# An RWKV-7 / latent-attention / ConvGLU step on one core: sums over a head's channels from split operands, and the final state transposed together with the samples' states

## What is computed

```python
kk = (k * k_k).reshape(B, T, H, N)
kk = kk * lax.rsqrt(jnp.maximum(jnp.sum(kk * kk, axis=-1, keepdims=True), 1e-12))
...
S_T, y = lax.scan(step, wkv0.astype(f32), ...)
mu = jnp.mean(y, axis=-1, keepdims=True)
var = jnp.mean(jnp.square(y - mu), axis=-1, keepdims=True)
y = ((y - mu) * lax.rsqrt(var + GN_EPS)).reshape(B, T, W) * lnx_g + lnx_b
```

## Time and profile before

| | |
|---|---|
| median of 3 runs | 2498.18 us (2497.25 to 2504.71) |
| the profiled execution | 2497.85 us, its span 2496.2 us |
| PE busy | 2431.5 us, 97% of the span |
| DVE busy | 1104.6 us, 44% |
| ACT busy | 870.8 us, 35% |
| mean granted clock of PE | 0.989 of full speed |
| DMA | 284.14 MB, 114 GB/s on average |

### The profile page before, as it was taken

One profiled execution on the slowest core, in us unless ns is written; L12 is line 12 of the kernel. 1 busy time (PEld: TensorE's weight loads), 2 busy tenths in 40 slices (PEclk: granted clock), 3 DMA queues, 4 the chain that ended last, 5 costly groups with the idle time before them and its releaser, 6 DMA issues.

```text
span 2496.2 us, 44147 instructions
## 1 busy us (share of the span) xinstructions
PE 2431.5 (97%) x17372; PEld 2232.2 (89%) x17372; DVE 1104.6 (44%) x1743; ACT 870.8 (35%) x1311; POOL 108.6 (4%) x182
## 2 busy tenths in 40 slices
PE   6999999999899999999998999999999999999997
PEld 6888888888899999999877999999878999999886
DVE  4555656654433322344333544444233444444234
ACT  4444344443323322344223433333222333333232
POOL 4000000000010100000000000000000000000010
PEclk9999999999999999999999999999999999999999
DMA  5323222222533433344533344444333444444433
GB/s 167 105 74 81 78 77 74 74 72 71 132 119 94 124 98 92 96 127 125 169 124 109 112 126 126 126 126 124 127 126 118 132 126 126 126 127 141 128 129 127
DMA packets 414538, 284.14 MB, mean 114 GB/s; under 512 B 31728, under 2 KB 392690, under 8 KB 413536
## 3 DMA queue, kind: packets, MB, share of 16 engines
q1 hardware_dynamic: 405600, 259.16, 35.3%
q0 software_dynamic: 8832, 23.36, 3.4%
HBM read 275.55 MB, written 6.92 MB: 113 GB/s over the span
## 4 chain that ended last, share of the span: by engine, by line
PE 95%; DVE 2%; ACT 1%; DMA 1%; issue 1%; POOL 0%; DVEq 0%; SPq 0%; POOLq 0%; ACTq 0%
PE banks L1453 20%; PE banks L903 19%; PE banks L907 18%; PE banks L904 18%; PE banks L324 2%; PE banks L916 2%; PE banks L918 2%; PE banks L917 2%; PE banks L392 1%; PE banks L1316 1%; PE banks L472 1%; PE banks L1319 1%; PE banks L457 1%; PE banks L1414 1%; PE banks L485 0%
## 5 line engine op out<-in xcount | busy, mean ns | idle before, releaser
L893 DVE TENSOR_TENSOR w_lo<-w_raw,w_hi 128x1024 fp32r<-128x1024 f32 x482 | 590.1, 1225 | 964.5 <-ACT w_hi L888 964.2
L903 PE MATMUL banks<-x_hi,w_hi 128*128 128x384 f32 x2640 | 918.6, 348 | 8.3 <-DVE w_lo L893 8.3
L907 PE MATMUL banks<-x_hi,w_lo 128*128 128x384 f32 x2640 | 886.9, 336 | 0.0
L904 PE MATMUL banks<-x_lo,w_hi 128*128 128x384 f32 x2640 | 885.7, 335 | 0.0
L888 ACT ACTIVATE w_hi<-w_raw 128x1024 fp32r<-128x1024 f32 x482 | 511.3, 1061 | 1039.9 <-PE banks L907 595.5
L903 PEld LDWEIGHTS banks<-x_hi,w_hi 128*128 128x128 f32 x2640 | 497.6, 188 | 35.6 <-issue 11.9
L904 PEld LDWEIGHTS banks<-x_lo,w_hi 128*128 128x128 f32 x2640 | 498.5, 189 | 5.0 <-issue 0.3
L907 PEld LDWEIGHTS banks<-x_hi,w_lo 128*128 128x128 f32 x2640 | 497.6, 188 | 1.2 <-issue 1.2
L1453 PE MATMUL banks<-w_hi,act_hi 128*128 128x512 f32 x528 | 164.2, 392 | 4.6 <-DVE h_rows L2009 2.4
L1453 PE MATMUL banks<-w_lo,act_hi 128*128 128x512 f32 x528 | 164.2, 392 | 0.0
L1453 PE MATMUL banks<-w_hi,act_lo 128*128 128x512 f32 x528 | 163.2, 390 | 0.0
(11 more groups left out here) (401 smaller groups left out, 2294.4 us busy)
## 6 DMA issues: line engine op xcount, KB each, us to landing
w_raw<-in_w_ffn_in SPq DMA_DIRECT2D x176, 512.0 KB, 4.0
w_raw<-in_w_in SPq DMA_DIRECT2D x144, 512.0 KB, 3.8
w_raw<-in_w_ffn_down SPq DMA_DIRECT2D x88, 512.0 KB, 3.6
w_raw<-in_w_out SPq DMA_DIRECT2D x32, 512.0 KB, 3.6
w_raw<-in_w_o_a SPq DMA_DIRECT2D x16, 512.0 KB, 4.0
w_raw<-in_w_o_b SPq DMA_DIRECT2D x16, 512.0 KB, 3.9
w_raw<-in_w_in SPq DMA_DIRECT2D x20, 256.0 KB, 3.8
w_ukv_head<-in_w_ukv POOLq DMA_DIRECT2D x8, 512.0 KB, 3.9
```

The source lines that it names most:

```text
L893: nc.vector.tensor_tensor(lo[:, s], raw[:, s], hi[:, s].bitcast(F32), ALU.subtract).then_inc(lo_done, 1)
L903: nc.tensor.matmul(out, hi[:, s, k, :], xh[:, kt, :], start=kt == 0, stop=False)
L904: nc.tensor.matmul(out, hi[:, s, k, :], xl[:, kt, :], start=False, stop=False)
L907: last = nc.tensor.matmul(out, lo[:, s, k, :], xh[:, kt, :], start=False, stop=kt == 15)
```

## The change

1. The three sums over a head are made of two fp32r products each (`head_sums`), with `bon_r`, an fp32r copy of `BON` that DVE makes once, and with a high part (an ACT copy to fp32r) and a low part (a DVE subtraction) of what is summed. The split operands lie where `m_t`, `c_k` and `c_b` are. ACT counts its three copies of a group in `split_hi`; `kk_sq_done`, `y_raw_done` and `y_sq_done` are now given by DVE, behind the subtraction. Two of ACT's squares are linked, because a copy reads them.
2. The prompt's final state is transposed directly ahead of the samples' states, and its copy stands directly ahead of theirs in ACT's list. The waits for `s_out` and `s0_in` move from ahead of `pe_lora_g` to ahead of `pe_s0`.
3. The numbers of pieces behind `y_ps` are 2, 3, 2, 3, 2 in place of 1, 2, 2, 3, 4.

```diff
--- before.py
+++ after.py
@@ -204,7 +204,16 @@
         be = region("beta", [P, NT])
         kp_ = region("kappa", [P, NT])
         n_t, t_x, t_y, t_g = [region(n, [P, 6, 64]) for n in ("n_t", "t_x", "t_y", "t_g")]
-        t_f, m_t, c_k, c_b = [region(n, [P, 6, P]) for n in ("t_full", "m_t", "c_k", "c_b")]
+        t_f = region("t_full", [P, 6, P])
+        kk_off = top[0]
+        m_t = region("m_t", [P, 6, P])
+        y_off = top[0]
+        c_k = region("c_k", [P, 6, P])
+        var_off = top[0]
+        c_b = region("c_b", [P, 6, P])
+        kk_s = at("square_split", [P, 2, NT], kk_off, F32R)
+        y_s = at("y_split", [P, 2, NT], y_off, F32R)
+        var_s = at("y_square_split", [P, 2, NT], var_off, F32R)
         tok = region("tok_major", [P, 3, 3, P])
         ra = region("r_and_alpha", [P, 5, P])
         un_s = t_y[:, 0:2, :].rearrange("p i c -> p (i c)")
@@ -218,6 +227,7 @@
         so = region("s_out", [64, NB, P])
         st = region("state", [P, 64])
         sto = region("state_rows", [64, P])
+        bon_r = region("bones_r", [P, P], F32R)
         assert top[0] <= 229368, top[0]
         yb, yc, sq_y, rn_y = [t[:, :, :].rearrange("p u c -> p (u c)") for t in (t_g, t_y, n_t, t_x)]
 
@@ -379,9 +389,13 @@
             for k in range(2):
                 nc.tensor.matmul(ps[:, 5, 0:NT], wg[:, k, :], za[:, 2 + k, :], start=k == 0, stop=k == 1)
 
+        def head_sums(out, split):
+            nc.tensor.matmul(out, bon_r[:, :], split[:, 0, :], start=True, stop=False)
+            return nc.tensor.matmul(out, bon_r[:, :], split[:, 1, :], start=False, stop=True)
+
         def pe_kk_sum(f):
             nc.tensor.wait_ge(E("kk_sq_done"), f + 1)
-            nc.tensor.matmul(ps[:, 3, 0:NT], BON, sq[:, :], start=True, stop=True).then_inc(E("kk_sum_ps"), 1)
+            head_sums(ps[:, 3, 0:NT], kk_s).then_inc(E("kk_sum_ps"), 1)
 
         def pe_s0(f):
             for b in range(NB):
@@ -568,29 +582,29 @@
                     last = mm_(ps[heads(i), 5, tile_tok(t)], u_and_p[:, t, 0, heads(i)], c_b[:, 3 * i + t, :],
                                start=False, stop=True, skip_group_check=True)
             last.then_inc(E("y_ps"), 1)
-            pieces(1)
+            pieces(2)
             pe.wait_ge(E("state_done"), f * 4 + 4)
             pe.wait_ge(E("y_raw_done"), f + 1)
-            mm_(ps[:, 3, 0:NT], BON, yb, start=True, stop=True).then_inc(E("mean_ps"), 1)
-            transpose(ps[0:64, 2, 0:P], st[:, :]).then_inc(E("sp_t_ps"), 1)
-            pieces(2)
+            head_sums(ps[:, 3, 0:NT], y_s).then_inc(E("mean_ps"), 1)
+            pieces(3)
             pe.wait_ge(E("sd_done"), f + 1)
             pe.wait_ge(E("y_sq_done"), f + 1)
-            mm_(ps[:, 4, 0:NT], BON, sq_y, start=True, stop=True).then_inc(E("var_ps"), 1)
+            head_sums(ps[:, 4, 0:NT], var_s).then_inc(E("var_ps"), 1)
             if more:
                 pe_kk_sum(f + 1)
             pieces(2)
+            transpose(ps[0:64, 2, 0:P], st[:, :])
             for b in range(NB):
                 last = transpose(ps[0:64, 6 + b // 4, (b % 4) * P:(b % 4 + 1) * P], s0t[:, b, :])
             last.then_inc(E("sd_t_ps"), 1)
             if more:
-                pe.wait_ge(E("s_out"), f + 1)
-                pe.wait_ge(E("s0_in"), f * 32 + 64)
                 pe_lora_g(f + 1)
             pieces(3)
             if more:
+                pe.wait_ge(E("s_out"), f + 1)
+                pe.wait_ge(E("s0_in"), f * 32 + 64)
                 pe_s0(f + 1)
-            pieces(4)
+            pieces(2)
 
         def act_gate_sigmoids(f):
             fn = nc.scalar.activation
@@ -599,9 +613,10 @@
             fn(sw[:, :], ps[:, 2, 0:NT], ACT.Sigmoid, bias=pf[:, 3:4])
             fn(aa[:, :], ps[:, 3, 0:NT], ACT.Sigmoid, bias=pf[:, 4:5]).then_inc(E("sig_done"), 1)
 
-        def act_kk_square(f):
+        def act_kk_square(f, ch):
             nc.scalar.wait_ge(E("kk_raw_done"), f + 1)
-            nc.scalar.activation(sq[:, :], kk0[:, :], ACT.Square).then_inc(E("kk_sq_done"), 1)
+            ch.link(nc.scalar.activation(sq[:, :], kk0[:, :], ACT.Square))
+            nc.scalar.activation(kk_s[:, 0, :], sq[:, :], ACT.Copy).then_inc(E("split_hi"), 1)
 
         def act_exps_early(f):
             fn = nc.scalar.activation
@@ -666,19 +681,18 @@
             act.wait_ge(E("u_ps"), f * 3 + 2)
             fn(un_s[:, :], ps[:, 3, 0:P], ACT.Copy, scale=-1.0).then_inc(E("u_done"), 1)
             if more:
-                act_kk_square(f + 1)
+                act_kk_square(f + 1, ch)
             cut(4)
             if more:
                 act_exps_early(f + 1)
             act.wait_ge(E("yd_ps"), f + 1)
             act.wait_ge(E("y_ps"), f + 1)
-            fn(yb, ps[:, 5, 0:NT], ACT.Copy).then_inc(E("y_raw_done"), 1)
+            fn(yb, ps[:, 5, 0:NT], ACT.Copy)
+            fn(y_s[:, 0, :], ps[:, 5, 0:NT], ACT.Copy).then_inc(E("split_hi"), 1)
             act.wait_ge(E("y_centred"), f + 1)
-            fn(sq_y, yc, ACT.Square).then_inc(E("y_sq_done"), 1)
+            ch.link(fn(sq_y, yc, ACT.Square))
+            fn(var_s[:, 0, :], sq_y, ACT.Copy).then_inc(E("split_hi"), 1)
             cut(5)
-            act.wait_ge(E("sp_t_ps"), f + 1)
-            act.wait_ge(E("states_stored"), OPEN + f)
-            fn(sto[:, :], ps[0:64, 2, 0:P], ACT.Copy).then_inc(E("s_out"), 1)
             if more:
                 act.wait_ge(E("sd_done"), f + 1)
                 act_exps_late(f + 1)
@@ -688,6 +702,8 @@
             if more:
                 act_kk_norm(f + 1, ch)
             act.wait_ge(E("sd_t_ps"), f + 1)
+            act.wait_ge(E("states_stored"), OPEN + f)
+            fn(sto[:, :], ps[0:64, 2, 0:P], ACT.Copy).then_inc(E("s_out"), 1)
             fn(so[:, :, :].rearrange("v (h b) c -> v h (b c)", h=2), ps[0:64, 6:8, :], ACT.Copy)\
                 .then_inc(E("so_done"), 1)
             cut(6)
@@ -737,6 +753,11 @@
         def dve_k_mod(ch):
             ch.link(nc.vector.tensor_scalar(t1[:, :], aa[:, :], -1.0, pf[:, 6:7], ALU.add, ALU.mult))
             ch.link(nc.vector.scalar_tensor_tensor(k2[:, :], t1[:, :], 1.0, z[:, 1, :], ALU.add, ALU.mult))
+
+        def dve_kk_low(f, first=False):
+            nc.vector.wait_ge(E("split_hi"), 1 if first else f * 3 - 1)
+            nc.vector.tensor_tensor(kk_s[:, 1, :], sq[:, :], kk_s[:, 0, :].bitcast(F32), ALU.subtract)\
+                .then_inc(E("kk_sq_done"), 1)
 
         def dve_clamp(f):
             nc.vector.wait_ge(E("kk_sum_ps"), f + 1)
@@ -851,10 +872,16 @@
             tt(s0t[:, :, :], s0t[:, :, :],
                e1[:, 256 + TS - 1:NT:TS].unsqueeze(2).to_broadcast([P, NB, 64]), M).then_inc(E("sd_done"), 1)
 
+            dve.wait_ge(E("split_hi"), f * 3 + 2 + more)
+            tt(y_s[:, 1, :], yb, y_s[:, 0, :].bitcast(F32), S).then_inc(E("y_raw_done"), 1)
+            if more:
+                dve_kk_low(f + 1)
             dve.wait_ge(E("mean_ps"), f + 1)
             stt3(yc, ps[:, 3, 0:NT], -1.0 / 64, yb, M, A).then_inc(E("y_centred"), 1)
             if more:
                 dve_k_mod(ch)
+            dve.wait_ge(E("split_hi"), f * 3 + 3 + more)
+            tt(var_s[:, 1, :], sq_y, var_s[:, 0, :].bitcast(F32), S).then_inc(E("y_sq_done"), 1)
             cut(5)
             if more:
                 dve_kappa(f + 1)
@@ -1550,7 +1577,7 @@
             act_gate_sigmoids(0)
             nc.scalar.preload_act_table_set("natural_log_exp_and_others")
             act_next(T_FT + 2)
-            act_kk_square(0)
+            act_kk_square(0, ch)
             act_exps_early(0)
             act_exps_late(0)
             taken_mixed(T_FT + 2, 2)
@@ -1849,11 +1876,13 @@
             dve_next(T_FT + 1)
             dve_key(0, ch)
             dve.wait_ge(E("tables_in"), 16)
+            cp(bon_r[:, :], BON)
             dve_scan(0, ch)
             dve_centre(ch)
             dve_excl()
             dve_k_mod(ch)
             dve_next(T_FT + 2)
+            dve_kk_low(0, True)
             dve_kappa(0)
             dve_clamp(0)
             dve_bonus_rho(0, ch)
@@ -2085,7 +2114,7 @@
                     ts(ht[:, t, 0:1024], ht[:, t, 0:1024], stat[:, t:t + 1], None, M).then_inc(E("y_ready"), 1)
 
 
-LINKS = {"act_rwkv": 2, "dve_rwkv": 16, "dve_ffn": 3}
+LINKS = {"act_rwkv": 4, "dve_rwkv": 16, "dve_ffn": 3}
 
 _INS = ["x_prompt", "x_sample", "cache_mla_latent", "cache_mla_krope", "state_rwkv_wkv", "state_rwkv_shift",
         "state_ffn_conv", "g_mix", "w_in", "mu_shift", "w0", "w2", "a0", "a2", "g2", "k_k", "k_a", "r_k", "lnx_g",
```

## The result

The changed kernel takes 2547.43 us (2544.97 to 2547.83, 4 runs) where the kernel before takes 2500.39: a ratio of 1.0185, 95% interval 1.0166 to 1.0204. The profiled execution took 2544.97 us against 2497.85, so the two profiles differ by 47.1 us. Forecast were 2525.5 and a range up to 2538: the direction is right, the size is 22 us short, and the time lies 9 us above the range.

The account below looks back on a forecast made before the run. PE, carrying 95% of the chain of waits and gapless in the head groups, was taken as the bound. 7 x 3.5 + 3.2 - 0.3 = 27.4 us on 2497.85 gave 2525.3, as median 2525.5 us; range 2517 to 2538.

Parts of the forecast that it names:

- The new order makes two stalls of 2 us: PE waits 2.0 us at piece 24, 2.1 at piece 28, first of new weight blocks, for their low parts.
- the 0.2 for restarting: In each head group, PE loses 0.2 us for restarting twice, behind the two stalls.
- The sums are worth 0.87 us a group: Three sums over a head on PE each go from 0.64 to 0.35 us, saving 0.87 a group.
- The state's transpose is worth nothing: On PE it takes 0.11 us wherever it stands, so moving it gains nothing by itself.
- A group +3.5, the last +3.2: Each of seven head groups gets 3.5 us longer; the last 3.2, between 2.5 and 3.6.
- Mine are 2.0 and 2.1, so the nearest row speaks against it: Head-group stalls of 2.0 and 2.1 us resemble a 2.2 us wait with clock at 1.00, arguing against clock falls.
- The fall of the clock: Rival: PE's clock falls in the stalls, once per head group, 8 x 1.7 = 13 us more, 2538; chance 0.09.
- the 2.2 us row: Profile row of PE's 2.2 us wait on act_lo, around which the clock stays at 1.00.
- Only one stall: Rival: only one of the head groups' two stalls appears, about 2.2 us less in each group, 2508; chance 0.06.
- a cover that holds: Rival: pieces 24 and 28 find their low parts ready, only the 7 us saving remains, 2491; chance 0.05.
- sums that don't shorten: Rival: new products run like half an old sum, 0.32 us, saving gone, +7, 2532; chance 0.06.
- What would show it: Signs: about fifteen 2 us PE waits on w_lo, 69.2 us groups, sum products 0.175 apart, clock at 1.00.

Follow-up runs that it names:

- 2: Kernel before with only the new order of pieces and of the state's transpose, keeping the old float32 sums: 2541.45 us, ratio 1.0161.
- 4: Changed kernel with the cuts that make the high and low parts for pieces 24 and 28 moved earlier on ACT and DVE: 2493.16 us, ratio 0.9968.
- 8: Changed kernel with piece 24's high part and piece 28's cut made earlier, and one piece moved to the group's end: 2480.36 us, ratio 0.9922.
- 9: Same order as 8, but with the old float32 sums and without the added copies and subtractions: 2485.69 us, ratio 0.9945.
- 3: Kernel before with only the state's transpose, its copy and the two waits moved: 2501.22 us, ratio 1.0011.
- 5: Changed kernel with only the cut for piece 24 moved earlier on ACT and DVE, leaving the second stall: 2515.97 us, ratio 1.0065.
- 11: Unaltered repeat of the changed kernel with only the cut for piece 28 moved earlier on ACT and DVE: 2511.23 us.
- 10: The changed kernel run once more, unaltered: 2542.64 us.
- 7: Changed kernel with one piece moved back to behind the variance sum (2, 2, 3, 3, 2): 2528.51 us, ratio 1.0124.

## Why the prediction was right or wrong

*The new order makes two stalls of 2 us.* Right, in place, size and releaser: 1.98 and 2.03 for 2.0 and 2.1, both on w_lo, with the low parts within 0.1 us of the times summed. These idle times count from the recorded end of the product before. From start to start, as the prediction counted, pieces 24 and 28 come 2.13 us (230.53 less 228.22 and 0.175) and 2.19 us (241.50 less 239.14 and 0.175) late, 0.1 more each than summed; with the 0.2 for restarting and the sums' -0.90 that makes the 3.6. Experiments 2 and 4 show it from both sides: the order alone brings the stalls, the cuts alone take them away.

*The sums are worth 0.87 us a group.* Right: 0.90 between experiments 8 and 9. *The state's transpose is worth nothing.* Right (3).

*A group +3.5, the last +3.2.* Right: 3.6 and 3.4. In the last one the load that sets the end starts at 671.94 and takes as long as in the earlier trace rows:

```profile
671.94 10.41 DMA w_raw<-in_w_in
```

*"Mine are 2.0 and 2.1, so the nearest row speaks against it."* This is the step that failed. The fall of the clock had been seen as a rival, with its mechanism and its price, and got a chance of 0.09 and one fall in each group; there were twelve in eight groups, 16.9 us on the path, and with them my sum gives 2525.3 + 16.9 = 2542.2 against 2544.97. The error was to read one occurrence as a bound. A single 2.2 us wait with the clock at 1.00 could not exclude falls behind sixteen like it, and in the next profile the clock fell behind that same wait. With a fall at 3.0 and none at 2.2 in two rows, a stall of 2.0 repeated sixteen times wanted, as I would put it now, a chance of some falls near one half and a range to 16 falls, 25 us. And the 2.2 us row was not all that the profile of the kernel before had to say: behind the head groups it has two waits of 1.7 and 1.8 us in a row, both shorter than the new stalls, and the clock fell there.

```profile
684.28 0.55 PE L324 MATMUL banks<-consts_all,k_rope_t 128*128 128x128 f32 x3 [1.71 <-DVE k_rope_t L1882]
686.59 1.11 PE L324 MATMUL banks<-consts_all,w_ukv_head 128*128 128x128 f32 x4 [1.76 <-ACT k_rope_rows L1616]
...
684.00:692.00 8.00, 5.95 (x21) 5.00 (x22) 0.23 (x1) 3.21 (x4) 2.57 (x4) 0.61 0.33 113
```

A mean of 0.61 over these 8 us is 3.1 us of clock lost. These two waits are in all thirteen profiles, and in nine the clock fell beside them. The Trainium skill ("TensorE: Matmul & The Clock Gate", section "Why this matters for your kernels") warns against idle gaps between bursts, but only against gaps longer than any that the head groups have here. There the clock fell at 46 of 72 gaps of 1.97 to 2.87 us, and behind none of 1.42 us or less.

*The other rivals.* Only one stall, a cover that holds, and sums that don't shorten: none of them is in the trace. *What would show it*: fifteen waits on w_lo (sixteen with the last group's), yes; "a group of 69.2" and "the clock at 1.00", no.

What stays open is what decides between falls and no falls at one and the same stall: alternation in 5, repetition in 11, change in 10. No run here was made to tell that apart.

## What to carry to other kernels

When fillers are moved between dependent steps, follow the numbered filler that opens a new block, not the number of fillers: here two of them slid ahead of the work of the other engines that feeds them, and the cure was to move that feeding with them. Price a repeated PE stall near 2 us at its length plus a chance of a clock fall, 1.5 us each here, never take that chance from one occurrence, and look at every wait of like length in the profile that you have. A shorter operation on a gapless engine is worth its length only if the engines that feed it keep their distance: the split sums were worth 7 us, and alone they brought a loss of 0.3 us a group.

## What had not been expected of the hardware

In the head groups the granted clock falls at idle gaps of 1.97 to 2.03 us in 41 of 67 occurrences (strictly in turn where one such gap comes every 67.5 to 69 us, experiment 5) and at all five gaps of 2.87 us; never in 48 groups without such a gap. Each fall costs 1.7 us of clock, and six of the 46 twice that (three in experiment 7, two in 2, one in 5). One and the same gap elsewhere in the program falls or not from profile to profile: the one of 2.2 us on act_lo in 8 of 13, one of 2.2 us on w_lo near 31 us in 3 of 13. It also falls with PE busy without a gap: four to eight times over 850 to 1060 us in all profiles but one, and not at all in that one, which makes up to some 12 us between executions whose code there is the same.
